# Three column blocks through the first phase of each FFN, a 12-slot ring for the first modulation slices, and SiLU of c ahead of the small loads

## The reference

```python
c_act = jax.nn.silu(c)
mod = c_act @ w_ada[l] + b_ada[l]                  # w_ada is 2048 x 18432
sh1, sc1, g1, sh2, sc2, g2, sh3, sc3, g3 = jnp.split(mod, N_MOD, axis=-1)
hn = _modulate(_rms(h, norm_ffn1[l]), sh1, sc1)    # x * (1 + scale) + shift
h = h + 0.5 * g1 * _swiglu(hn, ffn1_w1[l], ffn1_w3[l], ffn1_w2[l])
h = h + g2 * _mixer(_modulate(_rms(h, norm_mix[l]), sh2, sc2), ...)
h = h + 0.5 * g3 * _swiglu(_modulate(_rms(h, norm_ffn2[l]), sh3, sc3), ffn2_w1[l], ...)
# _swiglu(x) = (silu(x @ w1) * (x @ w3)) @ w2, with d_ff = 5632
```

## Time and profile before

| | us |
|---|---|
| median of 3 runs | 2686.64 |
| lowest and highest run | 2685.14 and 2687.61 |
| the profiled execution, first to last instruction (span) | 2683.7 |
| TensorE busy | 2539.3 |
| VectorE busy | 1826.7 |
| ScalarE busy | 1139.7 |
| moved by DMA | 609.87 MB, 227 GB/s over the span |

### The profile page before, as it was taken

The page is one execution under the profiler, slowest core; times in us unless marked ns, Lnnn a source line. Parts: engine busy times, 40 slices in busy tenths (PEclk is TensorE's granted clock), DMA queues, the critical chain, the costliest instruction groups (busy, mean ns, idle before and its releaser), DMA issues.

```text
span 2683.7 us, 34690 instructions
## 1 busy us (share of the span) xinstructions
PE 2539.3 (95%) x12514; PEld 2142.0 (80%) x12514; DVE 1826.7 (68%) x2088; ACT 1139.7 (42%) x1387; POOL 66.3 (2%) x67
## 2 busy tenths in 40 slices
PE   1499999999999799999999999999799999999998
PEld 1378888888887799889788888888588888888886
DVE  6878675757575788876786576766678555555555
ACT  3143444444343555554445443443444444444442
POOL 0000000000000200000010000000210000000000
PEclk9799999999999899999999999999899999999999
DMA  9979787878785677755354587877488666666664
GB/s 329 326 272 319 233 270 230 268 230 269 230 270 172 226 259 267 269 171 150 110 172 129 178 280 253 272 256 238 149 303 312 200 190 190 191 189 189 190 191 149
DMA packets 279977, 609.87 MB, mean 227 GB/s; under 512 B 23426, under 2 KB 24004, under 8 KB 278980
## 3 DMA queue, kind: packets, MB, share of 16 engines
q1 hardware_dynamic: 277648, 600.78, 69.3%
q10 hardware_dynamic: 1700, 4.58, 0.5%
q0 software_dynamic: 528, 3.17, 0.3%
HBM read 604.24 MB, written 4.22 MB: 227 GB/s over the span
## 4 chain that ended last, share of the span: by engine, by line
PE 88%; DVE 7%; DMA 2%; issue 1%; ACT 1%; POOL 0%; ACTq 0%; DVEq 0%; POOLq 0%
PE psum L1671 25%; PE psum L1672 25%; PE psum L1673 25%; PE psum L1821 3%; PE psum L1822 3%; PE psum L1823 3%; PE psum L1844 2%; DVE ada_acc L1070 2%; DMA ada_raw<-in_w_ada 2%; PE psum L1659 2%; PE psum L1678 1%; DVE w_lo L1043 1%; DVE y L1305 0%; DVE h L1308 0%; DVE y L1241 0%
## 5 line engine op out<-in xcount | busy, mean ns | idle before, releaser
L1043 DVE TENSOR_TENSOR w_lo<-raw,w_hi 128x1024 fp32r<-128x1024 f32 x850 | 1036.1, 1222 | 619.9 <-ACT w_hi L667 617.7
L667 ACT ACTIVATE w_hi<-raw 128x1024 fp32r<-128x1024 f32 x850 | 897.4, 1060 | 1051.9 <-PE psum L1673 977.5
L1671 PE MATMUL psum<-w_hi,xT_hi 128*128 128x512 f32 x1984 | 787.5, 397 | 16.6 <-issue 8.3
L1673 PE MATMUL psum<-w_hi,xT_lo 128*128 128x512 f32 x1984 | 775.6, 391 | 0.0
L1672 PE MATMUL psum<-w_lo,xT_hi 128*128 128x512 f32 x1984 | 775.4, 391 | 0.0
L1671 PEld LDWEIGHTS psum<-w_hi,xT_hi 128*128 128x128 f32 x1984 | 374.6, 189 | 98.2 <-issue 12.8
L1673 PEld LDWEIGHTS psum<-w_hi,xT_lo 128*128 128x128 f32 x1984 | 374.1, 189 | 79.1
L1672 PEld LDWEIGHTS psum<-w_lo,xT_hi 128*128 128x128 f32 x1984 | 374.5, 189 | 75.6
L1070 DVE SCALAR_TENSOR_TENSOR ada_acc<-ada_raw,cact,ada_acc 128x1024 f32<-128x1024 f32 x270 | 346.3, 1283 | 21.1 <-DMA ada_raw<-in_w_ada 17.3
L1671 PE MATMUL psum<-w_hi,aT_hi 128*128 128x512 f32 x704 | 278.5, 396 | 5.5 <-DVE aT_lo L1227 5.0
L1672 PE MATMUL psum<-w_lo,aT_hi 128*128 128x512 f32 x704 | 278.9, 396 | 0.0
(11 more groups left out here) (223 smaller groups left out, 1797.1 us busy)
## 6 DMA issues: line engine op xcount, KB each, us to landing
raw<-in_ffn_w SPq DMA_DIRECT2D x528, 512.0 KB, 4.5
ada_raw<-in_w_ada SPq DMA_DIRECT2D x288, 512.0 KB, 5.6
raw<-in_w_in SPq DMA_DIRECT2D x224, 512.0 KB, 3.8
raw<-in_w_br_ssd SPq DMA_DIRECT2D x32, 512.0 KB, 5.4
raw<-in_w_br_att SPq DMA_DIRECT2D x32, 512.0 KB, 4.6
raw<-in_w_out SPq DMA_DIRECT2D x32, 512.0 KB, 5.1
h<-in_x SPq DMA_DIRECT2D x1, 2048.0 KB, 8.9
gate_ffn<-gate_rows POOLq DMA_DIRECT2D x2, 1024.0 KB, 7.0
```

Of the source, the lines that this page charges most:

```text
L667: nc.scalar.activation(w_hi[:, n.slot(SPLIT), 0:size], raw[:, n.slot(RAW), 0:size], ACT.Copy).then_inc(hi_ready, 1)
L1043: nc.vector.tensor_tensor(w_lo[:, n.slot(SPLIT), 0:size], raw[:, n.slot(RAW), 0:size], w_hi[:, n.slot(SPLIT), 0:size], ALU.subtract).then_ ...
L1671: nc.tensor.matmul(o, hi[:, kt + k, toks], whi, start=a, stop=False)
L1673: ins = nc.tensor.matmul(o, lo[:, kt + k, toks], whi, start=False, stop=b)
```

## The change

**Three column blocks in the first phase.** The first phase now takes x@w1 of block 1 along: 24 units, for each pair j one of w1, one of w3, and one of w1's next block, which sums in banks 6 and 7. The low part has 12 units (`LOW`), the high part 12. A new step `second` of 16 units follows it: x@w3 of block 1 in banks 4 and 5, then the w2 product of block 0 in banks 2, 0, 2 and 4. From then on the kernel goes as before, with a `hidden` whose product is already made (`after_second`). FFN2 is changed in the same way. The number of units stays.

**The ring.** The first 64 slices go through 12 slots, 4 of `ada_raw` and 8 of a new `ada_more`. `early` loads 16 units beside them instead of 12, and the first four units come after slice 22 instead of slice 3. `ada_first` splits 16 units instead of 12 before the high part.

**SiLU of c** is issued after the first small load, ahead of the 16 others.

```diff
+ADA_DEEP = 12
+    ada_more = place("ada_more", at_temp + 52 * KB, [ADA_DEEP - ADA_RING, ADA_COLS])
-    FIRST = 2 * UPB
-    FIRST_ORDER = [(w, j) for low in (0, UPB // 2) for w in range(2) for j in range(low, low + UPB // 2)]
-    W1_DONE = UPB + UPB // 2
+    FIRST = 3 * UPB
+    FIRST_ORDER = [(w, j) for j in range(UPB) for w in range(3)]
+    FIRST_BANK = (0, 2, 6)
+    LOW = FIRST // 2
+    W1_DONE = FIRST - 2
+    SECOND = 2 * UPB
+    SECOND_BANKS = (2, 0, 2, 4)
...
 # ada_slot: the load of slice m waits for slice m - 12
+        if m.n0 < first:
+            return m.n0 % ADA_DEEP, m.n0 // ADA_DEEP + 1, m.n0 + 1 - ADA_DEEP if m.n0 >= ADA_DEEP else None
...
 # SyncE
-        early = {ADA_RING - 1: range(0, RAW)}
+        early = {22: range(0, RAW), 39: range(4, 6), 41: range(6, 8), 43: range(8, 9), 44: range(9, 10), 47: range(10, 11)}
+        early.update({49 + 2 * i: range(11 + i, 12 + i) for i in range(5)})
...
 # ScalarE
         act.dma_start(c_row[0:KT, :], c[0].rearrange("(r n) -> r n", n=P)).then_inc(c_in, 16)
+        act.wait_ge(c_ready, 1)
+        nc.scalar.activation(cact[:], vecT[:, 0:KT], ACT.Silu).then_inc(cact_ready, 1)
...
+            def second(n, o):
+                for u in range(SECOND):
+                    cast_units(n.n0 + u + 1)
+                    if u == 4:
+                        act.wait_ge(unit_done, n.n0)
+                        silu(o + 1, FIRST_BANK[2])
+                    if u == 7:
+                        act_hi(o, 0)
...
 # VectorE
+            m = e * KT + k
+            if 38 <= m < 50 and m % 2 == 1:
+                sub_units(6 + (m - 37) // 2)
+            if m in (55, 58, 61, 63):
+                sub_units(13 + (55, 58, 61, 63).index(m))
...
+            def second(n, o, adds):
+                for u in range(SECOND):
+                    sub_units(n.n0 + u + 1)
+                    ada_peeled(f)
+                    if u == 2:
+                        prod(o, n)
+                    if u == 7:
+                        act_lo(o, 0)
+                    if u == 10:
+                        prod(o + 1, n + UPB, 4)
+                    if u in (12, 14):
+                        q = (u - 12) // 2
+                        y_add(adds + q, q, n + (UPB + 2 * q + 2), SECOND_BANKS)
...
+                    if after_second and u in (0, 2):
+                        q = 2 + u // 2
+                        y_add(At(Y_ADDS[f] + q), q, n + (2 * q + 2 - UPB), SECOND_BANKS)
...
 # TensorE
-                if f == 0 and u == UPB:
+                if f == 0 and u == LOW:
                     sum_first(2)
                     sum_first(3)
...
+            def second(n, o, adds, ada):
+                for u in range(UPB):
+                    if u == 5:
+                        turn_act(o, 0)
+                    unit(n + u, xT_hi, xT_lo, 2 * u, 4, u == 0, u == UPB - 1)
+                for q in range(QB):
+                    if q == 0:
+                        pe.wait_ge(alo_ready, o.count(plus=1))
+                    if q == 2:
+                        pe.wait_ge(y_added, (adds + 1).count())
+                        pe.wait_ge(silu_ready, o.count(plus=2))
+                        pe.wait_ge(ada_used, (ada.n0 + 1) * KT)
+                        sum_ada(6, ada_acc[ada.n0 % 2])
+                    if q == 3:
+                        pe.wait_ge(prod_ready, o.count(plus=2))
+                    for k in range(2):
+                        unit(n + (UPB + 2 * q + k), aT_hi, aT_lo, 2 * k, SECOND_BANKS[q], k == 0, k == 1)
```

More of the change, by code:

```diff
@@ L245, in build @@
     unit_done = sem("unit_done")
-    ada_in = [sem(f"ada_in{k}") for k in range(ADA_RING)]
+    ada_in = [sem(f"ada_in{k}") for k in range(ADA_DEEP)]
     ada_used = sem("ada_used")
@@ L430, in ada_slot, with ada_row @@
     def ada_slot(m):
-        merge, ffn2 = ADA_MERGE * KT, ADA_FFN2 * KT
+        first, merge, ffn2 = ADA_FIRST * KT, ADA_MERGE * KT, ADA_FFN2 * KT
+        if m.n0 < first:
+            return m.n0 % ADA_DEEP, m.n0 // ADA_DEEP + 1, m.n0 + 1 - ADA_DEEP if m.n0 >= ADA_DEEP else None
+        deep = (first + ADA_DEEP - 1) // ADA_DEEP
         if m.n0 < merge:
-            return m.n0 % ADA_RING, m.count(each=ADA_RING, plus=1), m.count(plus=1 - ADA_RING) if m.n0 >= ADA_RING else None
+            return m.n0 % ADA_RING, (m + -first).count(each=ADA_RING, plus=deep + 1), m.count(plus=1 - ADA_RING)
+        landed = deep + (merge - first) // ADA_RING
         if m.n0 < ffn2:
-            return 2 + m.n0 % 2, (m + -merge).count(each=2, plus=merge // ADA_RING + 1), m.count(plus=-1)
+            return 2 + m.n0 % 2, (m + -merge).count(each=2, plus=landed + 1), m.count(plus=-1)
         slot = m.n0 % ADA_RING
-        before = merge // ADA_RING + ((ffn2 - merge) // 2 if slot >= 2 else 0)
+        before = landed + ((ffn2 - merge) // 2 if slot >= 2 else 0)
         return slot, (m + -ffn2).count(each=ADA_RING, plus=before + 1), max(m.n0 + 1 - ADA_RING, ffn2)
+    def ada_row(slot):
+        return ada_raw[:, slot, :] if slot < ADA_RING else ada_more[:, slot - ADA_RING, :]
     def ada_at(i):
@@ L776, in hidden @@
                         silu(o + 1)
-            for e in range(2):
-                hidden(At(n0 + FIRST + e * BLOCK), At(o0 + e))
+            second(At(n0 + FIRST), At(o0))
+            hidden(At(n0 + FIRST + SECOND), At(o0 + 1))
             with act.Fori(0, TRIPS) as trip:
@@ L1270, in hidden @@
                         y_add(adds + q, q, n + (UPB + 2 * q + 2))
-            for e in range(2):
-                hidden(At(n0 + FIRST + e * BLOCK), At(o0 + e), At(Y_ADDS[f] + e * QB))
-                mod_out(At((ADA_FIRST, ADA_FFN2)[f] + e), 6)
+            second(At(n0 + FIRST), At(o0), At(Y_ADDS[f]))
+            mod_out(At((ADA_FIRST, ADA_FFN2)[f]), 6)
+            hidden(At(n0 + FIRST + SECOND), At(o0 + 1), At(Y_ADDS[f] + QB), after_second=True)
+            mod_out(At((ADA_FIRST, ADA_FFN2)[f] + 1), 6)
             with dve.Fori(0, TRIPS) as trip:
@@ L1754, in ffn, with hidden @@
                     pe.wait_ge(xlo_ready, UPB * 2 * f + j + 1)
-                unit(At(n0 + u), xT_hi, xT_lo, 2 * j, 2 * w, j == 0, j == UPB - 1)
-            def hidden(n, o, adds, mods=None, ada=None):
+                unit(At(n0 + u), xT_hi, xT_lo, 2 * j, FIRST_BANK[w], j == 0, j == UPB - 1)
+            def second(n, o, adds, ada):
[15 more added lines that the diff above has]
+                        unit(n + (UPB + 2 * q + k), aT_hi, aT_lo, 2 * k, SECOND_BANKS[q], k == 0, k == 1)
+            def hidden(n, o, adds, mods=None, ada=None, after_second=False):
                 pe.wait_ge(silu_ready, o.count(plus=1))
+                if after_second:
+                    pe.wait_ge(y_added, (adds + -2).count())
                 for u in range(UPB):
@@ L1785, in ffn @@
             ada0 = (ADA_FIRST, ADA_FFN2)[f]
-            for e in range(2):
-                hidden(At(n0 + FIRST + e * BLOCK), At(o0 + e), At(Y_ADDS[f] + e * QB), At(ada0 + e), At(ada0 + e))
+            second(At(n0 + FIRST), At(o0), At(Y_ADDS[f]), At(ada0))
+            hidden(At(n0 + FIRST + SECOND), At(o0 + 1), At(Y_ADDS[f] + QB), At(ada0 + 1), At(ada0 + 1), after_second=True)
             with pe.Fori(0, TRIPS) as trip:
```

70 lines of the change are left out of this document (32 added, 38 removed).

## The result

| | before | after |
|---|---|---|
| median | 2686.11 us (2685.14 to 2687.61, 4 runs) | 2667.72 us (2665.55 to 2668.52, 4 runs) |
| ratio | | 0.9936 (95% interval 0.9924 to 0.9947) |
| span of the profiled execution | 2683.7 us | 2666.8 us |
| first modulation out | 72.39 us | 65.52 us |
| end of slice 63, TensorE sums | 133.13 us | 125.60 us |

The change saves 18.4 us in the medians, where 20.3 were forecast: 1.9 less. The time is only 1.4 us above the forecast of 2666.3, since the median of before is 2686.11 us here, over four runs, and was 2686.64 over the three that the forecast started from. In the two profiled executions the change saves 16.9 us: 7.5 ahead of the high part and 9.4 behind it. The profiled execution of after was the slowest of its four, 2668.52 us, 1.7 above its span.

A forecast was written before the change was run, and what follows sets the result against it. TensorE bounds FFN1 from the high part on; before it, loads and VectorE's slices do. 10.9 + 9.4 + 0 = 20.3 us off span 2683.7 gives 2663.4, plus 2.9 to the median: 2666.3 us; 8-in-10 range 2662 to 2677.

The forecast's parts named there:

- What bounds: FFN1 runs on TensorE's time once its high part begins; gains come only before 139.32 us or from fewer units behind.
- Term 1: Low part of FFN1: four more units (12 for 8) run ahead of the high part, saving 10.9 us.
- Term 2: First interval, to the first modulation: loads at 400 GB/s bring it out at 63.0 us, not 72.39, saving 9.4 us.
- Term 3: Second interval, first modulation to the end of slice 63: 60.7 us as before, so 0 us.
- The cover: Second interval: loads end ahead of VectorE's need, with 7 us left after some 3 us of pauses.
- At no cost: Sums, mods and clock ramp unchanged; later small loads, VectorE's work in `second` and FFN2's new order add no time.
- SiLU of c: Start of the kernel: VectorE starts near 4.3 us, not 10.67, but then waits for loads; worth nothing.
- `second`: Step of 16 units: VectorE's 41 us of work fits beside over 44 us, so its adds and products hide.
- A: Rival: loads are the bound, at 343 GB/s; only 11.2 us saved, 2675.4 us; chance 0.16.
- B: Rival: the load rate stays at 284 GB/s whatever is queued; slice 63 ends 14.8 us late, 2690.5 us; chance 0.05.
- C: Rival: VectorE falls behind in `second`, ten steps in both FFNs cost 27 us, 2693 us; chance 0.02.
- The rate of 358 GB/s: Rule against the forecast: a load takes 1.46 us, first-interval gain 4.3 us, time 2671.4; counted within the forecast's 0.75.

The follow-up runs named there:

- e_ring_only: The kernel before with the 12-slot ring, its order of loads and SiLU of c first, phases of two blocks: 2674.34 us, ratio 0.9959.
- e_silu_late: The changed kernel with SiLU of c issued behind the small loads again: 2667.56 us, ratio 0.9933.
- e_phase_only: The changed kernel with its ring cut to 4 slots, order of loads kept: 2690.73 us, ratio 1.0022.
- e_phase_mid: The changed kernel with a ring of 4 and units' loads moved: first four behind slice 3, units 4 to 7 behind slices 33 to 36: 2676.24 us.
- e_x_late: The changed kernel with the first four units loaded behind slice 31, their splits moved to suit, and `x` behind slice 15: 2662.66 us, ratio 0.9917.
- e_ring8: The changed kernel with 8 slots in place of 12: 2667.20 us, ratio 0.9935.

## Why the prediction was right

**What bounds.** FFN1 runs on TensorE's time from the high part on: right. All differences between the kernels arose ahead of the high part or by the number of units left behind it.

**Term 1, 10.9 us.** Right: the two kernels with a phase of two blocks have a rest of 2544.4 us, the ten with three blocks have 2531.9 to 2535.1, on average 2533.4, 11.0 less. After's own trace shows 9.4, where 10.9 were forecast. It had lost 0.5 us of the 10.9 by the last modulation sum of FFN1, 0.8 in FFN1's tail and 0.2 in the mixer. The first two go with a lower granted clock than before had in the same stretches (below); the prediction held the clock to be equal. After's four executions differ by 3.0 us in their spans, and the profiled one is the slowest; so its 9.4 says less about the change than the 11.0 of ten kernels.

**Term 2, 9.4 us.** The mechanism was right, the size was not: it measured 6.9. Slice 23 was priced to land at 44.9 us and VectorE took it at 46.82; the way from there to the first modulation is 18.7 us, and was summed to 18.1; slice 24 had to be waited for too (0.66 us). The sum also has a slip: its printed 59.6 and 3.66 us make 63.3, not 63.0, so that term 2 by its own prices was 9.1. The lateness is there at slice 9, 22.81 for 20.3. From 2 us on until slice 23 was there the mean rate was 392 GB/s:

```profile
2.00:46.80 44.80, 9.61 (x44) 8.17 (x45) 30.39 (x36) 13.89 (x27) 2.12 (x3) 1.00 1.02 392
```

Against a constant 400 that is 0.9 of the 1.9 us: the first 5 us at 206 GB/s and the two windows at 370 and 374. The other 1.0 us is bytes, by an estimate from the same line: 17.6 MB had moved, and the 32 loads with the small ones are 17.2, so 0.4 MB belonged to loads behind slice 23, which were partly done already. The prediction had read its price from windows with full queues. The trace of before has slower ones too, at the start and at the landing of `x`, and they could have been used:

```profile
0.00:5.00 5.00, 0.26 (x1) 0.18 (x1) 0.17 (x1) 0.00 (x0) 1.27 (x10) 1.00 0.60 205
...
20.00:25.00 5.00, 0.00 (x0) 0.00 (x0) 4.69 (x7) 0.00 (x0) 0.00 (x0) 1.00 0.98 370
```

**Term 3, 0 us.** It measured 0.7: 125.60 - 65.52 = 60.1 us against 60.7. By e_ring_only this is a difference of two sizes: the ring alone takes 3.7 us out of the second interval, and the four units more put 3.1 back. The split of unit 4 waited 1.29 us for 1.8. The cover was mis-sized, 2.9 us where I worked out 7; it held all the same. It also held with 8 slots. The two misses of terms 2 and 3, 2.5 us too much and 0.7 too little, offset each other in part, and that is luck.

**At no cost.** SiLU of c: nothing, as forecast (e_silu_late). FFN2: 0.0. `second`: no wait of TensorE between 131.79 us and the tail but 2.6 us at the start of the high part, which before has too. That the parts aren't independent the prediction didn't say. Term 1 stands only where the unit loads fit the ring: with after's own order and a ring of 4 it turns into a loss (e_phase_only), with another order 8.3 us are won (e_phase_mid). The ring alone is worth 10.4 us in the medians; with the 8.3 that is 18.7, against 18.4 for both together. But the 8.3 is not the phase alone: e_phase_mid has SiLU of c first too, its first modulation comes at 71.01 us for before's 72.39, and what SiLU is worth with a ring of 4 was not tried. That SiLU is worth nothing is shown for the ring of 12.

**Rivals.** A (343 GB/s) fell: it had slice 23 at 52 us, which came at 46.82, and the mean over 40 to 80 us is 393. B (284) fell with it. C (VectorE behind in `second`) fell: no wait in it. The rate of 358 GB/s that the Trainium skill, "DMA: Bandwidth & Descriptors", section Bandwidth, gives for streaming with both cores of a pair did not bind here with one core: 401 to 413 in most windows, and 2667.72 us lies below the 2671.4 worked out by it.

## What to carry to other kernels

A load that waits for a slot, put into an in-order queue, holds up everything behind it; put too late, it holds up its own user. Work out for each such load after which use its slot comes free and before which use it is needed, and set it between; with a deeper ring of its neighbours a late place did no harm here, and 8 slots were as good as 12. When streams share a queue, put first what the chain needs next: here four units moved behind the first modulation's last slice gave 5 us on top of the change, while an earlier start of VectorE gave nothing, since a wait for loads stood behind it. Price a load from windows of its own stretch, the first ones and the slow ones too, and count that a load is not done when its bytes would be: those behind it are under way.

## What the runs showed of the hardware

**Small loads behind a deep queue.** In before `pos_col`, 1 KB, was issued on ScalarE's queue at 8.64 us and landed some 8 us later. In after it was issued at 11.47 and landed at 28.12, 16.6 us later, beside several slices of 512 KB and the 2 MB of `x` from SyncE. ScalarE waited 14.9 us for it, with `x` there since 21.2 us. The same load took 9.9 us in e_phase_mid and 13.8 in e_phase_only, both with 4 slots, 14.3 in e_x_late, and 16.6 with 8 slots (e_ring8).

**The clock after a pause.** TensorE's granted clock has two levels, 0.50 (1.2 GHz) and 1.00 (2.4 GHz); a figure between them is a window that holds both. At the tail of FFN1 TensorE waits 1.3 and then 2.5 us for VectorE and goes on at the lower level; how long differs between the profiled executions. Windows of 4 us there (clock third from the end), before:

```profile
842.00:846.00 4.00, 2.52 (x7) 2.01 (x8) 3.86 (x5) 2.94 (x4) 0.00 (x0) 0.78 0.91 279
846.00:850.00 4.00, 4.00 (x15) 3.21 (x14) 0.83 (x1) 1.06 (x1) 0.00 (x0) 0.79 0.93 346
```

and after:

```profile
824.00:828.00 4.00, 2.44 (x6) 1.95 (x7) 3.78 (x5) 3.02 (x4) 0.01 (x1) 0.50 0.86 299
828.00:832.00 4.00, 4.00 (x13) 3.11 (x12) 0.91 (x1) 0.90 (x1) 0.00 (x0) 0.65 0.96 324
```

The same work ran at 0.50 and 0.65 where it had run at 0.78 and 0.79, and cost 0.8 us. The start of the high part, behind TensorE's wait of 17.4 us and the sums at the lower level, is a second such place. After and e_ring8 do the same there, and their first 20 us of it are

```profile
131.80:151.80 20.00, 20.00 (x75) 16.22 (x76) 15.85 (x18) 6.98 (x8) 0.00 (x0) 0.85 0.72 243
```

```profile
131.50:151.50 20.00, 19.96 (x81) 16.34 (x82) 16.60 (x19) 7.63 (x8) 0.00 (x0) 0.91 0.75 259
```

75 matmuls for 81, 0.85 for 0.91; before has 0.87. Of the 2.5 us by which after's rest is longer than e_ring8's, 1.2 are lost there, 0.8 in the tail of FFN1 and 0.5 in the mixer. The rest spreads over 3 us between the ten kernels whose work behind the high part is the same, and the spans of after's own four executions spread as far, 2663.8 to 2666.8 us. What sets when the clock rises was not tried.
